# Scan input and output, attention scores and probabilities times values as row or column tiles of the TensorE array

## Chip, cores and metric

The kernel runs on one core of one Trainium2 chip. The metric is the device time in microseconds, the median of the runs shown. All times here are microseconds unless marked ns.

## What is computed

Two layers of a decoder trunk over 256 tokens of width 1024, in float32. Each layer has a SwiGLU feed-forward block (hidden width 2816), then three token mixers that are fed by one projection, then a second feed-forward block, with a layer norm after each of the three. What the change touches lies in two of the mixers:

```python
# state-space mixer: 16 groups of 16 channels, 64 complex states each
bu_re = jnp.einsum('bsgc,gpc->bsgp', uf, bbar_re)      # input of the scan
bu_im = jnp.einsum('bsgc,gpc->bsgp', uf, bbar_im)
_, _, xs_re, xs_im = lax.associative_scan(combine, (aa_re, aa_im, bu_re, bu_im), axis=1)
y = (jnp.einsum('bsgp,gcp->bsgc', xs_re, c_re)          # output of the scan
     - jnp.einsum('bsgp,gcp->bsgc', xs_im, c_im))
...
# sliding-window attention: 8 query heads, 2 key/value heads, head size 64, blocks of 128 tokens
scores = jnp.einsum('bnqhgd,bnkhd->bnhgqk', qb, kk)
...
out = jnp.einsum('bnhgqk,bnkhd->bnqhgd', probs, vv)
```

## The kernel before

The weights come from HBM in chunks of 1 MB into three raw slots, in the order in which they are used, on SyncE's queue. ScalarE (ACT) rounds each chunk to a high part (L710), VectorE (DVE) makes the remainder (L1056), and TensorE (PE) multiplies three times (high by high, high by low, low by high; `project`, L426 to L428, for projections, `accumulate`, L441, for products that sum over the hidden width). A chunk of the projection is 48 matmuls of 256 moving columns. PE's order of work is written out by hand, and each chunk waits for its low part (`take`) and for ACT to have read the PSUM bank that it writes.

The parts of the mixers stand between the chunks of the projection in PE's list. They are plain float32 matmuls, each of which the trace shows as two pairs of a weight load and a matmul record. Their order in one layer is: scores (L606 for the block with a predecessor, 8 matmuls of 256 columns; L610 for the first block, 8 of 128 columns), chunks CC and HH, input 0, BB, chunk 7, input 1, chunk 8, output 0, chunk 9, input 2, transposes of the probabilities, chunk 10, output 1, `attend(1)`, chunk 11, input 3, transposes, chunk 12, output 2, `attend(0)`, chunks 13 and 14, output 3, chunk 15, and the gate of the state-space mixer.

The scan runs over 16 groups of channels, two to a "state tile" of 128 partitions, so eight state tiles; they are done two at a time (q from 0 to 3). `input_states(q)` (L554) makes 4 matmuls: for state tile t and the real or imaginary part, the stationary operand `bTz[:, t, ri, :]` has 128 rows of channels of which only 32 are not zero, and `uT` moves 256 tokens; the results go to PSUM bank 0 or 1. ACT copies them to `bu` (L826), DVE turns them (`turned_parts`, L1275 and L1276), scans (L1295) and turns them back into `sw` (L1304, L1305). `output_states(q)` (L564) makes 4 matmuls that add into one half of bank 2, with `cTz[:, t, ri, :]` stationary, of whose 128 columns only 32 are not zero. ACT may copy the states of q only when `sw` of q-1 is made, and PE waits for `sw` before output q.

For the scores a query tile `qT[:, m, :]` holds two heads, m in partitions 0 to 63 and m+4 in 64 to 127, and `kz` holds the keys of each of the two key heads with zeros in the other half, so 128 rows are multiplied of which 64 count. DVE scales and masks the scores (L1312), reduces them and makes the negative bound (L1359); ACT takes the exponentials (L879); GpSimd (POOL) normalises; PE transposes the probabilities. `attend(blk)` (L588) multiplies `vz[:, kb, j, :]`, which has the values of key head j in 64 of its columns and zeros in the rest, by the transposed probabilities of 128 queries, and sums over both key heads and one or two key blocks: 16 matmuls for block 1, 8 for block 0. ACT reads each gate chunk of the projection out of PSUM with a sigmoid (L818).

Of the kernel before, what the change touches and what calls it, by code (L numbers as in the profile page):

```python
# [27 lines left out]
P = 128  # L28
DEPTH, D, SEQ, DFF = 2, 1024, 256, 2816
# [20 lines left out]
HD, HEADS = 64, 8  # L50
# [55 lines left out]
def trunk(nc, x, ffn1_w_gate, ffn1_w_up, ffn1_w_down, ln1_g, ln1_b, w_in, conv_w, conv_b,  # L106
# [4 lines left out]
    with ctx:  # L111
        def sb(name, shape, dt=F32):
            return ctx.enter_context(nc.sbuf_tensor(name, shape, dt))

        def overlay(first, second):

            size = [sum(4 * math.prod(shape[1:]) for _, shape, _ in s) for s in (first, second)]
            held, brief = (second, first) if size[1] >= size[0] else (first, second)
            with ExitStack() as own:
                over = [own.enter_context(nc.sbuf_tensor(*a)) for a in brief]  # L120
            kept = [sb(*a) for a in held]
            return over + kept if held is second else kept + over
# [13 lines left out]
        probsT, rows_hi, rows_lo = overlay(  # L136
            [("probsT", [P, 2 * HEADS, P], F32)],
            [("rows_hi", [P, 2, 2, SEQ], F32R), ("rows_lo", [P, 2, 2, SEQ], F32R)])
# [7 lines left out]
        bTz, y_cs = overlay([("bTz", [P, STATE_TILES, 2, P], F32)], [("y_cs", [P, 4, 2, SEQ], F32R)])  # L146
# [4 lines left out]
        qT, cv_c, cv_h = overlay([("qT", [P, 4, SEQ], F32)], [("cv_c", [P, 2, SEQ], F32), ("cv_h", [P, 2, SEQ], F32)])  # L151
        kz = sb("kz", [P, 2, SEQ])
        vz = sb("vz", [P, 2, 2, P])
# [11 lines left out]
        sw = sb("sw", [P, 2, 2, SEQ])  # L165
        tp = sb("tp", [P, 2, 2, SEQ])
        k_tok = sw[:, 0, :, 0:P]
        uT = sb("uT", [P, 2, SEQ])
        cTz = sb("cTz", [P, STATE_TILES, 2, P])
# [23 lines left out]
        ps = ctx.enter_context(nc.psum_tensor("ps", [P, 8, 512], F32))  # L193
# [215 lines left out]
        def _(pe):  # L409
            mm = nc.tensor.matmul  # L410
# [98 lines left out]
            with pe.Fori(0, DEPTH) as l:  # L509
# [9 lines left out]
                for u in range(2):  # L519
                    for ri in range(2):  # L520
                        n = (2 * u + ri) * P
                        nc.tensor.transpose(ps[:, 0, n:n + P], b_blk[:, ri, 4 * u:4 * u + 4, :], ident[:, :])
                        last = nc.tensor.transpose(ps[:, 1, n:n + P], c_in[:, u, ri, :, :], ident[:, :])
# [24 lines left out]
                def input_states(q):  # L548

                    if q >= 1:  # L550
                        pe.wait_ge(bu_made.sem, bu_made.at(l, q))
                    for t in range(2 * q, 2 * q + 2):
                        for ri in range(2):
                            last = mm(ps[:, t % 2, ri * SEQ:ri * SEQ + SEQ], bTz[:, t, ri, :], uT[:, t // 4, :],  # L554
                                      start=True, stop=True)
                    last.then_inc(bu_done.sem, 1)

                def output_states(q):

                    pe.wait_ge(x_state_made.sem, x_state_made.at(l, q + 1))  # L560
                    ct = q // 2
                    for t in range(2 * q, 2 * q + 2):
                        for ri in range(2):
                            last = mm(ps[:, 2, ct * SEQ:ct * SEQ + SEQ], cTz[:, t, ri, :], sw[:, ri, t % 2, :],  # L564
                                      start=t % 4 == 0 and ri == 0, stop=t % 4 == 3 and ri == 1)
                    last.then_inc(c_done.sem, 1)

                def transpose_probs(S, parts, g0, first):
# [11 lines left out]
                def attend(blk):  # L580

                    pe.wait_ge(pT_made.sem, pT_made.at(l, 4 if blk else 6))
                    for m in range(4):
                        terms = [(j, kb) for j in range(2) for kb in range(blk + 1)]
                        for n, (j, kb) in enumerate(terms):
                            head = m + 4 * j
                            i = 2 * head + kb if blk else head
                            last = mm(ps[:, 3, m * P:m * P + P], vz[:, kb, j, :], probsT[:, i, :],  # L588
                                      start=n == 0, stop=n == len(terms) - 1)
                    last.then_inc(pv_done.sem, 1)  # L590

                chunk(KV)
# [3 lines left out]
                for t in range(NT):  # L596
                    last = nc.tensor.transpose(ps[:, 2, t * P:t * P + P], k_tok[:, t, :], ident[:, :])
# [4 lines left out]
                pe.wait_ge(proj_read.sem, proj_read.at(l, QB + 1))  # L602
                pe.wait_ge(bcT_made.sem, bcT_made.at(l, 1))
                pe.wait_ge(kz_made.sem, kz_made.at(l, 1))
                for head in range(HEADS):
                    last = mm(ps[:, head // 2, (head % 2) * SEQ:(head % 2) * SEQ + SEQ],  # L606
                              qT[:, head % 4, P:2 * P], kz[:, head // 4, :], start=True, stop=True)
                last.then_inc(scores_done.sem, 1)
                for head in range(HEADS):
                    last = mm(ps[:, 6 + head // 4, (head % 4) * P:(head % 4) * P + P],  # L610
                              qT[:, head % 4, 0:P], kz[:, head // 4, 0:P], start=True, stop=True)
                last.then_inc(scores_done.sem, 1)
                chunk(CC)
                chunk(HH)
                pe.wait_ge(s_made.sem, s_made.at(l, 2))
                input_states(0)
                chunk(BB)
                chunk(7)
                input_states(1)
                chunk(8)  # L620
                output_states(0)
                chunk(9)
                input_states(2)
                pe.wait_ge(probs_made.sem, probs_made.at(l, 1))
                transpose_probs(S1, 4, 0, 0)
                chunk(10)
                output_states(1)
                attend(1)
                chunk(11)
                input_states(3)  # L630
                pe.wait_ge(probs_made.sem, probs_made.at(l, 2))
                transpose_probs(S0, 2, 4, 16)
                chunk(12)
                output_states(2)
                pe.wait_ge(ya_lo.sem, ya_lo.at(l, 1))
                attend(0)
                chunk(13)
                chunk(14)
# [5 lines left out]
                for co in range(2):  # L644
                    for c in range(2):
                        last = mm(ps[:, 0, co * SEQ:co * SEQ + SEQ], w_glu[:, c, co * P:co * P + P], sw[:, 0, c, :],
                                  start=c == 0, stop=c == 1)
# [819 lines left out]
```

## Time and profile before

| | |
|---|---|
| median of 3 runs | 1194.88 (1194.86 to 1196.68) |
| profiled execution | 1195.63, its span 1193.8 |
| busy: PE / DVE / ACT / POOL | 96% / 63% / 48% / 13% |
| mean granted TensorE clock | 0.984 of full speed |
| PE's stretch of the mixers, layer 0 / layer 1 | about 235 to 335 / 822 to 922 |
| HBM | 203.77 MB read, 172 GB/s over the span |

Busy time is the share of the span in which an engine runs an instruction. A matmul record lasts from its start until its last result is written, and the next one starts well before that, so the spacing of starts, and not the duration, is what a matmul takes. In a timeline a row with "x16" merges sixteen neighbouring instructions of one line. An amount in brackets is the idle time of the engine before the instruction and who ended it.

### The profile page before, as it was taken

To read this page: it belongs to the slowest core of one execution; us is meant where nothing else is said; L and a number is where in the kernel's file an instruction comes from. 1 tells how busy PE (TensorE), PEld (TensorE's weight loads), DVE (VectorE), ACT (ScalarE), POOL (GpSimd) and SP (SyncE) were. 2 spreads that over 40 slices of the span, in tenths; PEclk is the share of its full clock that TensorE was granted. 3 is DMA by queue.
4 is the path that set the end of the run, shared out by engine and by line. 5 is a ranking of instruction groups with operands and counts; after the bars stand their busy time and mean duration, and the time that the engine had idled before them with its cause. 6 is when DMAs were issued, how large, how long until landed. Compare 5 with 4: busy or idle time off the path is not lost.

```text
span 1193.8 us, 20955 instructions
## 1 busy us (share of the span) xinstructions
PE 1145.8 (96%) x8164; PEld 1082.6 (91%) x8166; DVE 753.7 (63%) x700; ACT 575.2 (48%) x652; POOL 154.1 (13%) x147
## 2 busy tenths in 40 slices
PE   5999999999999899999979999999999998999995
PEld 5999999999999799999879999989999988999994
DVE  4665447779948664544557544577897586644455
ACT  5565553863444544334356555455735435334331
POOL 2199000003000000000004950000300000000001
PEclk8999999999999899999989999999999998999998
DMA  7565567443466456556455655645445563555650
GB/s 223 181 211 189 192 200 193 155 129 117 139 178 200 153 177 190 195 176 215 139 157 178 207 176 189 232 107 177 141 135 153 174 219 126 191 178 187 197 177 35
DMA packets 176209, 205.60 MB, mean 172 GB/s; under 512 B 27012, under 2 KB 160792, under 8 KB 176152
## 3 DMA queue, kind: packets, MB, share of 16 engines
q1 hardware_dynamic: 175824, 204.76, 54.2%
q8 instruction: 36, 0.59, 0.2%
q14 instruction: 21, 0.17, 0.1%
q10 hardware_dynamic: 328, 0.08, 0.0%
HBM read 203.77 MB, written 1.05 MB: 172 GB/s over the span
## 4 chain that ended last, share of the span: by engine, by line
issue 79%; POOL 13%; PE 6%; ACT 1%; DVE 1%; POOLq 0%; ACTq 0%; DVEq 0%
POOL rot_c L1008 3%; POOL rot_s L1014 2%; POOL tp L1012 2%; POOL S L1022 2%; PE ps L428 1%; PE ps L427 1%; PE ps L426 1%; POOL tp L1010 1%; POOL tp L1004 1%; POOL tp L1006 1%; ACT S L879 1%; PE ps L606 1%; POOL rstd L988 1%; PE ps L543 0%; PE ps L544 0%
## 5 line engine op out<-in xcount | busy, mean ns | idle before, releaser
L1056 DVE TENSOR_TENSOR w_lo<-raw,w_hi 128x2048 fp32r<-128x2048 f32 x186 | 434.4, 2338 | 271.4 <-ACT w_hi L710 271.4
L426 PE MATMUL ps<-xT,w_hi 128*128 128x256 f32 x1984 | 568.1, 286 | 12.8 <-DVE xT L1102 12.8
L427 PE MATMUL ps<-xT,w_hi 128*128 128x256 f32 x1984 | 564.6, 285 | 0.0
L428 PE MATMUL ps<-xT,w_lo 128*128 128x256 f32 x1984 | 564.5, 285 | 0.0
L710 ACT CAST w_hi<-raw 128x2048 fp32r<-128x2048 f32 x186 | 353.4, 1902 | 155.1 <-PE ps L428 114.7
L426 PEld LDWEIGHTS ps<-xT,w_hi 128*128 128x128 f32 x1984 | 384.2, 194 | 17.3 <-DVE xT L1102 15.7
L427 PEld LDWEIGHTS ps<-xT,w_hi 128*128 128x128 f32 x1984 | 384.2, 194 | 1.7
L428 PEld LDWEIGHTS ps<-xT,w_lo 128*128 128x128 f32 x1984 | 383.9, 193 | 0.0
L441 PE MATMUL ps<-w_hi,rows_hi 128*128 128x512 f32 x416 | 130.8, 391 | 0.0
L441 PE MATMUL ps<-w_lo,rows_hi 128*128 128x512 f32 x416 | 130.4, 390 | 0.0
L441 PE MATMUL ps<-w_hi,rows_lo 128*128 128x512 f32 x416 | 130.2, 389 | 0.0
L988 POOL TENSOR_TENSOR rstd<-veps,mhalf 128x1 f32<-128x1 f32 x12 | 6.6, 550 | 815.3 <-DVE veps L1119 815.3
L441 PEld LDWEIGHTS ps<-w_lo,rows_hi 128*128 128x128 f32 x416 | 78.1, 188 | 16.7
L441 PEld LDWEIGHTS ps<-w_hi,rows_lo 128*128 128x128 f32 x416 | 78.1, 188 | 16.6
L721 ACT CAST rows_hi<-hid 128x512 fp32r<-128x512 f32 x44 | 27.3, 620 | 132.3 <-PE ps L441 98.2
L441 PEld LDWEIGHTS ps<-w_hi,rows_hi 128*128 128x128 f32 x416 | 75.3, 189 | 13.1
L715 ACT ACTIVATE act<-ps 128x512 f32<-128x512 f32 x44 | 26.3, 597 | 123.0 <-PE ps L428 122.9
L1069 DVE TENSOR_TENSOR rows_lo<-hid,rows_hi 128x512 fp32r<-128x512 f32 x44 | 32.7, 742 | 57.5 <-ACT rows_hi L721 57.4
L1064 DVE TENSOR_TENSOR hid<-act,ps 128x512 f32<-128x512 f32 x44 | 30.2, 687 | 49.1 <-PE ps L428 49.1
L818 ACT ACTIVATE gates<-ps 128x512 f32<-128x512 f32 x24 | 14.4, 598 | 80.6 <-PE ps L428 80.6
L768 ACT ACTIVATE xTf<-ps,ln_cur 128x128 f32<-128x128 f32 x72 | 27.0, 455 | 9.9 <-PE ps L456 9.9
L1008 POOL TENSOR_TENSOR rot_c<-tp 128x512 f32<-128x512 f32 (+6 forms) x18 | 31.7, 1759 | 1.4
(186 smaller groups left out, 930.4 us busy)
## 6 DMA issues: line engine op xcount, KB each, us to landing
raw<-in_ffn_w_gate SPq DMA_DIRECT2D x44, 1024.0 KB, 5.4
raw<-in_ffn_w_up SPq DMA_DIRECT2D x44, 1024.0 KB, 5.3
raw<-in_ffn_w_down SPq DMA_DIRECT2D x44, 1024.0 KB, 4.9
raw<-in_w_in SPq DMA_DIRECT2D x34, 1024.0 KB, 5.3
raw<-in_w_out SPq DMA_DIRECT2D x8, 1024.0 KB, 4.9
raw<-in_w_in SPq DMA_DIRECT2D x16, 256.0 KB, 4.5
raw<-in_w_br_attn SPq DMA_DIRECT2D x16, 256.0 KB, 4.6
gb<-in_ln_g SPq DMA_DIRECT2D x6, 512.0 KB, 5.3
```

The costliest lines, as they stand in the source:

```text
L426: mm(o, h[:, c, n], xT[:, c, 0, :], start=i == 0, stop=False)
L427: mm(o, h[:, c, n], xT[:, c, 1, :], start=False, stop=False)
L428: last = mm(o, w[:, c, n], xT[:, c, 0, :], start=False, stop=i == KC - 1)
L441: last = mm(acc[:, t, n, :], left[:, buf, c, tok], right[:, c, n * 512:n * 512 + 512], start=start and first and c == 0, stop=stop and lef ...
L710: nc.scalar.copy(w_hi[s][:, :], raw[s][:, :]).then_inc(hi_made.sem, 1)
L715: act_(act[:, :, :], ps[:, 4, :].rearrange("p (m t) -> p m t", m=2), ACT.Silu).then_inc(silu_made.sem, 1)
L721: nc.scalar.copy(rows_hi[:, buf], hid[:, :, :]).then_inc(h_hi.sem, 1)
L768: last = act_(xTf[:, c, t * P:t * P + P], ps[:, 6 - 2 * t + c // 4, (c % 4) * P:(c % 4 + 1) * P], ACT.Identity, scale=ln_cur[:, 2 * (norm_ ...
L1008: tt(rot_c[:, tl, n:2 * n], t0, t1, ALU.subtract).then_inc(pool_chain, 1)
L1056: tt(w_lo[s][:, :], raw[s][:, :], f32(w_hi[s][:, :]), ALU.subtract).then_inc(lo_made.sem, 1)
L1064: tt(hid[:, :, :], act[:, :, :], ps[:, 5, :].rearrange("p (m t) -> p m t", m=2), ALU.mult).then_inc(h_made.sem, 1)
L1069: tt(rows_lo[:, buf], hid[:, :, :], f32(rows_hi[:, buf]), ALU.subtract).then_inc(h_lo.sem, 1)
```

## The change

The zero parts of the operands are no longer multiplied. `input_states` and the scores take the 32 or 64 rows that count, as row tiles of the array; `output_states` and `attend` take the 32 or 64 columns that count, as column tiles. Two column tiles write different partitions of the same bank. The loops are reordered so that two neighbouring matmuls lie in different tiles: state tiles t and t+1 inside the real and the imaginary part; heads m and m+4 in turn; key heads inside key blocks. The count of matmuls and their moving columns stay as they were, and so do all waits and all other engines' work.

```diff
-                    for t in range(2 * q, 2 * q + 2):
-                        for ri in range(2):
-                            last = mm(ps[:, t % 2, ri * SEQ:ri * SEQ + SEQ], bTz[:, t, ri, :], uT[:, t // 4, :],
-                                      start=True, stop=True)
+                    for ri in range(2):
+                        for t in range(2 * q, 2 * q + 2):
+                            ch = slice(32 * (t % 4), 32 * (t % 4) + 32)
+                            last = mm(ps[:, t % 2, ri * SEQ:ri * SEQ + SEQ], bTz[ch, t, ri, :], uT[ch, t // 4, :],
+                                      start=True, stop=True, tile_position=(ch.start, 0))
                     last.then_inc(bu_done.sem, 1)
 
                 def output_states(q):
 
                     pe.wait_ge(x_state_made.sem, x_state_made.at(l, q + 1))
                     ct = q // 2
-                    for t in range(2 * q, 2 * q + 2):
-                        for ri in range(2):
-                            last = mm(ps[:, 2, ct * SEQ:ct * SEQ + SEQ], cTz[:, t, ri, :], sw[:, ri, t % 2, :],
-                                      start=t % 4 == 0 and ri == 0, stop=t % 4 == 3 and ri == 1)
+                    for ri in range(2):
+                        for t in range(2 * q, 2 * q + 2):
+                            ch = slice(32 * (t % 4), 32 * (t % 4) + 32)
+                            last = mm(ps[ch, 2, ct * SEQ:ct * SEQ + SEQ], cTz[:, t, ri, ch], sw[:, ri, t % 2, :],
+                                      start=ri == 0, stop=ri == 1, skip_group_check=True, tile_position=(0, ch.start))
                     last.then_inc(c_done.sem, 1)
...
                     for m in range(4):
-                        terms = [(j, kb) for j in range(2) for kb in range(blk + 1)]
-                        for n, (j, kb) in enumerate(terms):
+                        terms = [(j, kb) for kb in range(blk + 1) for j in range(2)]
+                        for j, kb in terms:
                             head = m + 4 * j
                             i = 2 * head + kb if blk else head
-                            last = mm(ps[:, 3, m * P:m * P + P], vz[:, kb, j, :], probsT[:, i, :],
-                                      start=n == 0, stop=n == len(terms) - 1)
+                            half = slice(HD * j, HD * j + HD)
+                            last = mm(ps[half, 3, m * P:m * P + P], vz[:, kb, j, half], probsT[:, i, :],
+                                      start=kb == 0, stop=kb == blk, skip_group_check=True, tile_position=(0, half.start))
                     last.then_inc(pv_done.sem, 1)
...
-                for head in range(HEADS):
+                by_pairs = [(m + 4 * j, slice(HD * j, HD * j + HD)) for m in range(4) for j in range(2)]
+                for head, half in by_pairs:
                     last = mm(ps[:, head // 2, (head % 2) * SEQ:(head % 2) * SEQ + SEQ],
-                              qT[:, head % 4, P:2 * P], kz[:, head // 4, :], start=True, stop=True)
+                              qT[half, head % 4, P:2 * P], kz[half, head // 4, :], start=True, stop=True,
+                              tile_position=(half.start, 0))
                 last.then_inc(scores_done.sem, 1)
-                for head in range(HEADS):
+                for head, half in by_pairs:
                     last = mm(ps[:, 6 + head // 4, (head % 4) * P:(head % 4) * P + P],
-                              qT[:, head % 4, 0:P], kz[:, head // 4, 0:P], start=True, stop=True)
+                              qT[half, head % 4, 0:P], kz[half, head // 4, 0:P], start=True, stop=True,
+                              tile_position=(half.start, 0))
```

## Rows read from the trace of the kernel before

**Rows 1.** The page: span, busy time by engine, busy tenths of DVE in 40 slices

```profile
span 1193.8 us, 20955 instructions
...
PE 1145.8 (96%) x8164; PEld 1082.6 (91%) x8166; DVE 753.7 (63%) x700; ACT 575.2 (48%) x652; POOL 154.1 (13%) x147
...
DVE  4665447779948664544557544577897586644455
```

**Rows 2.** The page: shares by engine of the chain that ended last

```profile
issue 79%; POOL 13%; PE 6%; ACT 1%; DVE 1%; POOLq 0%; ACTq 0%; DVEq 0%
```

**Rows 3.** Groups of PE by form: busy us, mean ns of one, idle before

```profile
L564 PE MATMUL ps<-sw,cTz 128*128 128x256 f32 x64 | 15.5, 386 | 0.9 <-DVE sw L1305 0.7
L554 PE MATMUL ps<-uT,bTz 128*128 128x256 f32 x64 | 15.1, 379 | 0.0
...
L588 PE MATMUL ps<-probsT,vz 128*128 128x128 f32 x96 | 11.4, 275 | 0.0
```

**Rows 4.** Timeline of PE at the scores, layer 0: start, duration, instruction

```profile
235.73 0.28 PE L428 MATMUL ps<-xT,w_lo 128*128 128x256 f32 x1
235.85 3.62 PE L606 MATMUL ps<-kz,qT 128*128 128x256 f32 x16
239.31 1.95 PE L610 MATMUL ps<-kz,qT 128*128 128x128 f32 x16
241.01 0.36 PE L426 MATMUL ps<-xT,w_hi 128*128 128x256 f32 x1
```

**Rows 5.** Timeline of PE at input 0, layer 0

```profile
252.60 1.89 PE L554 MATMUL ps<-uT,bTz 128*128 128x256 f32 x8
...
254.45 0.28 PE L427 MATMUL ps<-xT,w_hi 128*128 128x256 f32 x1
254.57 0.28 PE L428 MATMUL ps<-xT,w_lo 128*128 128x256 f32 x1
```

**Rows 6.** Timeline of PE at output 1 and attend(1), layer 0

```profile
290.54 0.28 PE L428 MATMUL ps<-xT,w_lo 128*128 128x256 f32 x1
290.92 1.99 PE L564 MATMUL ps<-sw,cTz 128*128 128x256 f32 x8
...
292.75 3.73 PE L588 MATMUL ps<-probsT,vz 128*128 128x128 f32 x32
296.24 0.36 PE L426 MATMUL ps<-xT,w_hi 128*128 128x256 f32 x1
```

**Rows 7.** Timeline of PE at output 3, layer 0

```profile
325.97 1.99 PE L564 MATMUL ps<-sw,cTz 128*128 128x256 f32 x8 [0.35 <-DVE sw L1305]
```

**Rows 8.** Timeline of DVE in the mixers, layer 0

```profile
249.03 0.17 DVE L1359 TENSOR_TENSOR esink<-sinks,negm 128x16 f32<-128x16 f32 x1
...
257.10 2.29 DVE L1056 TENSOR_TENSOR w_lo<-raw,w_hi 128x2048 fp32r<-128x2048 f32 x1 [5.34 <-ACT w_hi L710]
...
269.48 7.83 DVE L1056 TENSOR_TENSOR w_lo<-raw,w_hi 128x2048 fp32r<-128x2048 f32 x2
...
290.18 0.69 DVE L1305 TENSOR_TENSOR sw<-td,tp 128x512 f32<-128x512 f32 x1
...
309.03 2.28 DVE L1056 TENSOR_TENSOR w_lo<-raw,w_hi 128x2048 fp32r<-128x2048 f32 x1
313.97 1.23 DVE L1275 TENSOR_TENSOR td<-bu,rot_c 128x1024 f32<-128x1024 f32 x1 [2.66 <-ACT bu L826]
...
325.23 0.69 DVE L1305 TENSOR_TENSOR sw<-td,tp 128x512 f32<-128x512 f32 x1
```

**Rows 9.** Timeline of ACT in the mixers, layer 0

```profile
247.04 0.59 ACT L813 COPY cv_c<-ps 128x512 f32<-128x512 f32 x1 [8.61 <-PE ps L428]
...
249.45 1.28 ACT L879 ACT_TABLE_LOAD   x1
...
310.63 0.60 ACT L818 ACTIVATE gates<-ps 128x512 f32<-128x512 f32 x1 [5.00 <-PE ps L428]
```

**Rows 10.** After the norm between layers: busy by engine, granted clock; PE's timeline

```profile
600.00:610.00 10.00, 4.50 (x21) 4.50 (x22) 9.93 (x16) 7.88 (x10) 0.00 (x0) 0.67 0.40 112
...
605.88 0.41 PE L427 MATMUL ps<-xT,w_hi 128*128 128x256 f32 x1
606.09 0.41 PE L428 MATMUL ps<-xT,w_lo 128*128 128x256 f32 x1
```

## Prediction, made before the changed kernel ran

> **What bounds the kernel now.** I read the page's busy shares first: PE works 96% of the span and the others far less [rows 1]. So the question is whether a microsecond taken off PE's list comes off the end. The chain of waits doesn't settle it: 79% of it is "issue" [rows 2], PE going from one instruction to the next with nothing to wait for. It says only that PE's order of work is most of the chain. Then the groups of PE instructions: the changed lines have 256 matmul records (64 each for L554 and L564, 96 for L588, and 32 and 32 in two layers for L606 and L610) [rows 3, 4]. An fp32 matmul is two records, each a weight load and a pass. The timeline gives what they take. Sixteen passes of 256 columns run from 235.85 to 239.31, 0.216 each; sixteen of 128 columns from there to 241.01, 0.106 each [rows 4]. The durations in the groups (379 and 275 ns) are latencies of overlapping instructions and are not to be added up. Around an input group of eight passes, L554 starts at 252.60 and the second projection matmul at 254.45; without the group that would be at 252.72, so it costs 1.73, eight times 0.216 [rows 5].
>
> Per layer: eight state groups at 1.73 make 13.8, the scores 3.46 + 1.70 = 5.2, probabilities times values 48 passes of 0.107 = 5.2 (32 of them from 292.75 to 296.24 [rows 6]). That is 24.2 us a layer, 48.4 in all, 4% of the span: all that the change can touch.
>
> Last, what runs beside it. In this stretch DVE is at 9 tenths in two slices of each layer, nearly as full as PE [rows 1]. Its timeline has two idle stretches that matter: 5.34 before 257.10 and 2.66 before 313.97 [rows 8]; between 257.10 and 311.3 it never rests. PE, in its turn, waits for DVE: before the third output group 0.35 [rows 7], and it starts the second 0.26 late (L428 at 290.54, L564 at 290.92 where 290.66 was its turn) [rows 6]. So part of this stretch is bound by DVE's chain and PE's savings are partly lost there.
>
> **The change, part by part.**
>
> Overlap. The operands shrink from 128 partitions or columns to 32 or 64, but the moving columns stay, so a single pass costs what it did (0.216 or 0.107); any gain comes from two tiles running side by side. The program order is tile A pass 1, A pass 2, B pass 1, B pass 2, and matmuls start in order. A's second pass needs A's part of the array, so it waits for A's first; B's first can go beside A's second; B's second waits for B's first and shares its slot with the next A. So n matmuls of alternating tiles take n+1 slots and not 2n (nor n/2 or n/4, though four 32-row tiles exist: neighbours are only ever two tiles). Eight passes become 5 slots, sixteen become 9, thirty-two become 17. Saved: 3 x 0.216 = 0.65 for a state group; 7 x 0.216 + 7 x 0.107 = 1.51 + 0.75 for the scores; 15 x 0.107 = 1.60 for block 1 and 0.75 for block 0 of the values. Neighbours write different banks (row tiles) or different partitions (column tiles), so nothing else separates them.
>
> Switches. Nothing in the trace of before shows a change of tiling. The lower bound is nothing: from L554 to full-size projections there is no gap [rows 5]. The nearest rows for the upper bound are those of the pipeline: a full matmul is 0.28 long but 0.12 after its neighbour, so 0.16 would be laid bare if the array had to empty, and the eight passes after a wait take 1.99 where eight in a stream take 1.89, 0.10 for a weight load that could not be made ahead [rows 5, 6]. Two switches for a state group alone; one each for L610 and L606 (same tile shape, one stretch); three for an output group with its values stretch (32 columns, then 64, then full).
>
> Net on PE per layer: scores 1.51 + 0.75 - 0.52 = 1.74; each of six state groups that stand alone (four input, two output) 0.65 - 0.52 = 0.13; output 1 with block 1 0.65 + 1.60 - 0.78 = 1.47; output 2 with block 0 0.65 + 0.75 - 0.78 = 0.62. Sum 4.6 a layer, 9.2 in all.
>
> Weight loads. Two loads must now fit in a slot. Full loads are seen 0.12 apart (the projections) and here at 0.106 (L610) [rows 4]; two of them make 0.21 to 0.24, as long as a 256-column slot, but twice a 128-column slot. Row tiles keep 128 weight columns, so L610's 0.75 may be zero. That bound goes in the range; column tiles load 32 or 64 columns and are clear of it.
>
> What of it reaches the end. (1) Scores. The DVE waits for L606's last pass (saved 1.51 - 0.26 = 1.25), and ACT for the end of the projection after it, at 247.04 [rows 9] (saved 1.74). DVE's last step of the softmax bound is at 249.03 [rows 8], ACT's exponentials begin at 249.45 [rows 9], so ACT's side is 0.25 later; it leads by 0.5 less after, and the exponentials come about 1.45 earlier. They gate the copy and split that end DVE's idle time at 257.10, and DVE's chain is closed until 290.87, where it releases output 1. PE arrives there 1.74 + 4 x 0.13 = 2.3 early and gains 1.45: about 0.8 is lost as a longer wait before the second output group. The tightest DVE step under way is the rounded-off weights for the projection at 275: two of them take 269.48 to 277.31 [rows 8], so the first is done at 273.4, 1.6 ahead, more than that 0.8. (2) From output 1 to the fourth input: 1.47 + 0.13 = 1.60 ahead of DVE. ACT takes the gate at 310.63 as PE's projection ends, and then copies the last input states, for which DVE idles 2.66 [rows 8, 9]. That idle time covers the 1.60, so all of it counts. (3) From there DVE turns, scans and turns back until PE's third wait at 325.97 [rows 7, 8]: output 2 with block 0, 0.62, is lost. (4) Output 3, 0.13, counts, as PE is alone in front after it. Per layer 1.45 + 1.60 + 0.13 = 3.2; two layers 6.4 us.
>
> The clock. After some norms PE's granted clock is down to 1.2 GHz for a while (0.67 of full speed on average from 600 to 610, when PE had been idle) and matmuls then come 0.21 apart instead of 0.12 [rows 10]. Twenty such records after 605.88 cost 1.9. How many fall under it depends on where the norm lies against these stretches, and everything after 236 moves by microseconds. With five norms to come I allow 2.5 either way and nothing in the middle.
>
> The profiled execution took 1195.63, 1.8 over its span of 1193.8; the median of the three is 1194.88, 0.06% less. 1195.63 - 6.4 = 1189.2; from the median, 1188.5. I predict 1188.5.
>
> **The rivals.**
>
> R1, DVE sets the end. If switches are nearly free, PE runs ahead wherever it can. Then (1) is at most 1.9, (2) would be 0.65 + 1.60 + 0.65 = 2.9 but DVE's idle time ends at 2.66, (4) is 0.65: 5.2 a layer, 1184.5. For it: PE takes other shapes without a gap today. Against: those all use the whole array.
>
> R2, the pairs hardly overlap in the narrow groups, or switches cost some 0.5: then a state group loses 0.35 each, scores keep about 1.2, output 1 with block 1 keeps 0.75, and the sum over both layers is 0 to -2.4: 1192.5 to 1195. It decides where a switch passes 0.32, half of a state group's 0.65.
>
> R3, slower: no two passes overlap. If the second of the two passes holds the whole array, or fp32 passes are not spread over tiles, the slots stay 2n and all 20 switches of a layer are paid at 0.26: 5.2, less the waits before two output groups (0.26 and 0.35) that hide some, about 4.6 a layer, 9.2 in all: 1204. It decides at the first neighbour pair: L606's passes stay 0.216 apart. For it: today two records never run closer than their columns take. Against: today they always share the whole array. The Trainium skill (TensorE: Matmul & The Clock Gate, Part 3) gives 3.07 times for four row tiles of one-pass matmuls and 2.38 for three column tiles, which speaks against R3; no run here shows it for two passes.
>
> R4, the compiler ignores the positions and issues the same full matmuls: the order alone changes and the time is 1194.9. The smaller partitions in the instructions speak against it.
>
> **Chances.** Forecast 0.55, R1 0.12, R2 0.13, R3 0.17, R4 0.03. Within 0.2% (2.4 us, what a measurement of this kernel can tell from no change) lie R4, two thirds of R2, and a forecast upset by the clock. Of R2's rest and of a forecast upset by the clock, 0.02 each go to faster and to slower. Faster 0.67, same 0.14, slower 0.19. The range: R1 less 2 for the clock gives 1182.5; upwards the forecast, R2 and the lower edge of R3 (overlap missing, half of the switch price) give 1200.
>
> **What would show it.** In the profile after: L606 sixteen passes in about 1.9 instead of 3.46, L554 groups in 1.1 (start to start) instead of 1.73, a gap of about 0.26 on either side; PE's lateness before the second output group up from 0.26 to about 1.1, its wait before the last up by 0.6; DVE's idle time for the last input states down from 2.66 to about 1.1. The forecast fails if passes of neighbouring tiles keep the old spacing, if a switch costs over 0.32, or if DVE's idle time doesn't shrink.

## The result, and the profile after

The changed kernel takes 1180.95 (median of 4 runs, 1180.69 to 1182.07) against 1194.87 before (median of 4, 1192.04 to 1196.68). The ratio is 0.9887, with a 95% interval from 0.9867 to 0.9908: 1.1% faster. The profiled execution took 1181.15, with a span of 1179.3, so 14.5 less than the one of before. The forecast was 6.4 less and its range ended at 1182.5, so the measured time lies below the range: right in sign, and the forecast gain is less than half of the measured one.

The page shows PE with 20 us less busy time than in [rows 1], and DVE as it was:

```profile
span 1179.3 us, 20957 instructions
...
PE 1125.3 (95%) x8166; PEld 1055.3 (89%) x8166; DVE 753.4 (64%) x700; ACT 575.1 (49%) x652; POOL 154.0 (13%) x147
```

The timeline of PE at the scores, the counterpart of [rows 4] (L606 and L610 are now L610 and L615):

```profile
235.49 0.28 PE L428 MATMUL ps<-xT,w_lo 128*128 128x256 f32 x1
235.70 2.00 PE L610 MATMUL ps<-kz,qT 64*128 64x256 f32 x16
237.53 1.06 PE L615 MATMUL ps<-kz,qT 64*128 64x128 f32 x16
238.52 0.39 PE L426 MATMUL ps<-xT,w_hi 128*128 128x256 f32 x1
238.74 0.28 PE L427 MATMUL ps<-xT,w_hi 128*128 128x256 f32 x1
```

Sixteen passes of 256 columns went from 3.46 to 1.83, sixteen of 128 columns from 1.70 to 0.99. Read record by record, the passes start in pairs: 0.007 from the first of a pair to the second and 0.209 to the next pair, so 0.216 for two. The passes of 128 columns do the same, with 0.111 for two. So a slot of the prediction, the time of one pass, now holds two. Input 0, the counterpart of [rows 5] (L554 is now L555):

```profile
250.02 0.28 PE L428 MATMUL ps<-xT,w_lo 128*128 128x256 f32 x1
250.23 1.13 PE L555 MATMUL ps<-uT,bTz 32*128 32x256 f32 x8
251.29 0.38 PE L426 MATMUL ps<-xT,w_hi 128*128 128x256 f32 x1
251.51 0.28 PE L427 MATMUL ps<-xT,w_hi 128*128 128x256 f32 x1
```

From the last projection before the group (L428) to the second one after it (L427), 1.49 instead of 1.97. Four slots of 0.216 and the two regular steps of 0.12 make 1.10, so the two changes of tile shape cost 0.39 together, 0.19 each. They are seen as a start that comes 0.21 after L428 and not 0.12, a first pair that is held 0.10 longer, and the same two on the way back.

Output 1 with block 1, the counterpart of [rows 6]:

```profile
286.58 0.28 PE L428 MATMUL ps<-xT,w_lo 128*128 128x256 f32 x1
288.47 1.06 PE L566 MATMUL ps<-sw,cTz 128*32 128x256 f32 x8 [1.61 <-DVE sw L1311]
289.46 1.97 PE L591 MATMUL ps<-probsT,vz 128*64 128x128 f32 x32
291.36 0.39 PE L426 MATMUL ps<-xT,w_hi 128*128 128x256 f32 x1
```

The work from L566 to L426 takes 2.89, where L564 to L426 took 5.32. In front of it PE now idles 1.61 for DVE; before outputs 2 and 3 it idles 0.91 and 0.87. Another 0.5 of its lead goes before that, at the first transposes of the probabilities, where its idle time grows from 0.36 to 0.88. The timeline of DVE, the counterpart of [rows 8]:

```profile
247.27 0.18 DVE L1365 TENSOR_TENSOR esink<-sinks,negm 128x16 f32<-128x16 f32 x1
...
254.64 2.29 DVE L1062 TENSOR_TENSOR w_lo<-raw,w_hi 128x2048 fp32r<-128x2048 f32 x1 [4.98 <-ACT w_hi L716]
...
287.73 0.68 DVE L1311 TENSOR_TENSOR sw<-td,tp 128x512 f32<-128x512 f32 x1
...
306.58 2.28 DVE L1062 TENSOR_TENSOR w_lo<-raw,w_hi 128x2048 fp32r<-128x2048 f32 x1
308.78 1.22 DVE L1281 TENSOR_TENSOR td<-bu,rot_c 128x1024 f32<-128x1024 f32 x1
```

The 2.66 of idle time before the last turn are gone altogether: from 254.64 to 327 DVE has no pause. It is the bound of this stretch now.

Where the 14.5 went, by comparing the starts of the same instructions in the two traces:

| stretch | gain |
|---|---|
| to the scores of layer 0 | 0.15 |
| scores to the last gate (L818, now L824), layer 0 | 5.79 |
| from there to the scores of layer 1 | 1.32 |
| the same stretch in layer 1 | 5.80 |
| from there to the end | 1.42 |

So each layer gave 5.8, and 2.7 came where nothing was changed. The granted clock in windows of 6 us after the second norm of each layer (the one behind the mixers), before and then after. It is the third number from the end of a row, as a share of full speed:

```profile
404.00:410.00 6.00, 5.27 (x28) 4.70 (x27) 5.92 (x6) 4.22 (x4) 0.00 (x0) 0.60 0.15 15
991.00:997.00 6.00, 5.14 (x27) 4.73 (x27) 5.91 (x6) 4.17 (x4) 0.00 (x0) 0.59 0.11 16
```

```profile
397.00:403.00 6.00, 5.18 (x35) 4.05 (x35) 5.77 (x9) 5.44 (x8) 0.00 (x0) 0.90 0.01 3
977.00:983.00 6.00, 5.38 (x36) 4.07 (x34) 5.76 (x9) 5.29 (x7) 0.00 (x0) 0.88 0.01 3
```

Before, 15 and 16 projection matmuls came 0.21 apart there, at 1.2 GHz; after, none did. Each costs 0.093 more at that clock, and 31 times 0.093 is 2.9, near the 2.7. The clock falls at these norms in the changed kernel too, but there it is down only while the transposes and the zeroing of the sum banks run (0.50 from 395.0 to 398.2 in layer 0), and full again when the projection starts at 399.54.

### The profile page after: what moved, and what is told of

It reads as the page before. It is cut to its first block, busy times and chain, and to the rows that moved or that the text cites. A ratio compares the mean times of both kernels' runs of the same rounds, so it can differ in the third digit from the quotient of the medians.

```text
span 1179.3 us, 20957 instructions
## 1 busy us (share of the span) xinstructions
PE 1125.3 (95%) x8166; PEld 1055.3 (89%) x8166; DVE 753.4 (64%) x700; ACT 575.1 (49%) x652; POOL 154.0 (13%) x147
## 4 chain that ended last, share of the span: by engine, by line
issue 79%; POOL 13%; PE 6%; ACT 1%; DVE 1%; POOLq 0%; ACTq 0%; DVEq 0%
POOL rot_c L1014 3%; POOL rot_s L1020 2%; POOL tp L1018 2%; POOL S L1028 2%; PE ps L426 1%; PE ps L428 1%; PE ps L427 1%; POOL tp L1016 1%; POOL tp L1010 1%; POOL tp L1012 1%; ACT S L885 1%; POOL rstd L994 1%; PE ps L543 0%; PE ps L610 0%; PE ps L544 0%
## 5 line engine op out<-in xcount | busy, mean ns | idle before, releaser
L426 PE MATMUL ps<-xT,w_hi 128*128 128x256 f32 x1984 | 566.0, 285 | 12.6 <-DVE xT L1108 12.6
L427 PE MATMUL ps<-xT,w_hi 128*128 128x256 f32 x1984 | 563.1, 284 | 0.0
L428 PE MATMUL ps<-xT,w_lo 128*128 128x256 f32 x1984 | 563.1, 284 | 0.0
L426 PEld LDWEIGHTS ps<-xT,w_hi 128*128 128x128 f32 x1984 | 382.5, 193 | 20.2 <-DVE xT L1108 14.8
L427 PEld LDWEIGHTS ps<-xT,w_hi 128*128 128x128 f32 x1984 | 382.7, 193 | 1.5
L428 PEld LDWEIGHTS ps<-xT,w_lo 128*128 128x128 f32 x1984 | 382.4, 193 | 0.0
L824 ACT ACTIVATE gates<-ps 128x512 f32<-128x512 f32 x24 | 14.3, 598 | 73.9 <-PE ps L428 73.9
```

The lines of the kernel that those rows point to most:

```text
L426: mm(o, h[:, c, n], xT[:, c, 0, :], start=i == 0, stop=False)
L427: mm(o, h[:, c, n], xT[:, c, 1, :], start=False, stop=False)
L428: last = mm(o, w[:, c, n], xT[:, c, 0, :], start=False, stop=i == KC - 1)
```

## The experiments

Two questions were open: how the passes of different tiles run side by side, and what hands PE's gain on to the end. In the tables, "layer" is the gain against the profile of before in that stretch, from the first score matmul to the last gate, for layers 0 and 1, read in the experiment's own trace. The clock after the norms lies outside it. The runs of before were repeated beside each experiment, so their median differs a little from table to table.

### The tiles in the old order

The first hunk stands twice, in `input_states` and in `output_states`.

```diff
-                    for ri in range(2):
-                        for t in range(2 * q, 2 * q + 2):
+                    for t in range(2 * q, 2 * q + 2):
+                        for ri in range(2):
...
-                        terms = [(j, kb) for kb in range(blk + 1) for j in range(2)]
+                        terms = [(j, kb) for j in range(2) for kb in range(blk + 1)]
...
-                by_pairs = [(m + 4 * j, slice(HD * j, HD * j + HD)) for m in range(4) for j in range(2)]
+                by_pairs = [(m + 4 * j, slice(HD * j, HD * j + HD)) for j in range(2) for m in range(4)]
```

> The changed kernel with its tile positions, but the matmuls in the old order: both parts of a state tile, then the next state tile; heads 0 to 3, then 4 to 7; key blocks inside key heads. So runs of 4 (states, block 1 of the values) or 8 passes (scores) of one tile follow one another. In the changed kernel the passes start in pairs 0.007 apart and a pair takes 0.216 (256 columns). Theory F (free tiles): each tile works off its own passes, and program order holds only within a tile. Then the order is of no account, provided that PE looks far enough ahead: L610's sixteen passes still take 1.8, and the time is 1181 +- 1. Theory N (neighbours): a pass can run beside the one before it only. Then a state group takes 7 slots of 8 plus the switches and costs 0.15 more than before, the scores 15 of 16 slots, block 1 about 25 of 32: nothing is gained in the groups but 0.7 in block 1, and the time is 1194 to 1197.

Measured: 1186.28 (1184.36 to 1188.23) beside 1196.32 of the kernel before on the same chip, ratio 0.9914 (0.9893 to 0.9935); layer 4.85 and 4.83. Neither theory gave that. PE's timeline of this run, at input 0 and at the scores:

```profile
250.71 0.28 PE L428 MATMUL ps<-xT,w_lo 128*128 128x256 f32 x1
250.92 1.14 PE L555 MATMUL ps<-uT,bTz 32*128 32x256 f32 x8
251.99 0.39 PE L426 MATMUL ps<-xT,w_hi 128*128 128x256 f32 x1
```

```profile
235.43 2.32 PE L610 MATMUL ps<-kz,qT 64*128 64x256 f32 x13
237.37 0.37 PE L615 MATMUL ps<-kz,qT 64*128 64x128 f32 x1
237.58 0.38 PE L610 MATMUL ps<-kz,qT 64*128 64x256 f32 x1
237.59 0.38 PE L615 MATMUL ps<-kz,qT 64*128 64x128 f32 x2
237.80 0.38 PE L610 MATMUL ps<-kz,qT 64*128 64x256 f32 x1
237.81 0.38 PE L615 MATMUL ps<-kz,qT 64*128 64x128 f32 x2
```

The input group takes what it takes in the changed kernel (1.14 against 1.13), though four passes of one tile come before the first of the other. Theory N is out. At the scores, where eight passes of one tile come first, four run alone (starts 0.22 to 0.32 apart) and the ninth starts 0.007 after the fifth; from there two tiles are at work. The stretch takes 3.79 instead of 2.82, and that 0.97 is the 0.95 that this kernel's layer lacks against 5.80. The rows show even more: L615's passes (they are for the tile that got through first) start ahead of L610 passes that stand before them in the program. So a tile works off its own passes and other tiles don't hold it, within a limit: the ninth pass waits for the fifth, and L615's first, the seventeenth, starts 0.006 after the thirteenth. What the limit counts was not worked out; a plain count of four passes it is not, as the twenty-first starts at 237.92, ahead of the sixteenth at 238.01.

Theory F holds with that limit; its 1181 did not. The limit explains 1.9 of the 5.3 by which the median lies over the changed kernel's. By the traces the difference is 6.3, of which 4.4 lies outside the layers' stretches: after the second norms 16 and 18 projections came 0.21 apart again, and 1.4 was lost at the first norm of layer 1, where neither the kernel before nor the changed one met the lower clock.

### Row tiles alone, column tiles alone

The first has scan output and probabilities times values as before, the second has scores and scan input as before. Their diffs are the halves of the change.

> Row tiles alone (scan input and scores); scan output and probabilities times values as before. By the measured pieces, scores 2.2 less and an input group 0.5 less. Theory D (DVE's chain hands the scores' gain on, then DVE's idle time before the last input states hands on what PE gained since output 1): 2.2 + 0.5 = 2.7 a layer, 5.4 in all, 1189.5 at the same clock; DVE's idle time 2.66 -> 2.2. If PE alone set the end, it would be 2.2 + 4 x 0.5 = 4.2 a layer, 8.4 in all, 1186.5.

> Column tiles alone (scan output and probabilities times values); scores and scan input as before. By the measured pieces, output 1 with block 1 is 2.4 less, output 3 0.7 less, both in front of DVE or alone. Theory D: 2.4 + 0.7 = 3.1 a layer, 6.2 in all, 1188.7 at the same clock; DVE's idle time 2.66 -> 0.3. With rows_only it should add up to about the 11.4 that the two layers of the changed kernel gave, and what is over that (some 3) to neither, as it comes from the clock after the norms. If PE alone set the end, 2 x 0.5 + 2.4 + 1.5 = 4.9 a layer, 9.8 in all, 1185.

| | median | ratio (95%) | layer | DVE idle before the last turn |
|---|---|---|---|---|
| row tiles | 1188.03 | 0.9935 (0.9918 to 0.9952) | 2.83, 2.81 | 2.15 |
| column tiles | 1188.54 | 0.9939 (0.9922 to 0.9956) | 3.16, 3.16 | 0.24 |

DVE's timelines, row tiles and then column tiles:

```profile
311.24 1.22 DVE L1279 TENSOR_TENSOR td<-bu,rot_c 128x1024 f32<-128x1024 f32 x1 [2.15 <-ACT bu L830]
```

```profile
311.39 1.22 DVE L1277 TENSOR_TENSOR td<-bu,rot_c 128x1024 f32<-128x1024 f32 x1 [0.24 <-ACT bu L828]
```

Theory D gave 2.7 and 3.1 a layer and idle times of 2.2 and 0.3; PE alone would have given 4.2 and 4.9. Theory D stands, and the halves add up: 2.8 + 3.2 = 6.0, less 0.2 for DVE's idle time, which the two together would overdraw. The medians (8.3 and 7.8 under their own runs of before) are larger than 5.6 and 6.3. In both traces no projection after the second norms ran at 1.2 GHz, which is worth 2.7; the trace of the column tiles loses 1.4 of that at the first norm of layer 1, where its granted clock is 0.72 from 793 to 799 and that of before is full in the same work, 796 to 802.

### The normalisation of the probabilities on ACT

```diff
+                def scaled_probs(S, blk):
+                    for head in range(HEADS):
+                        last = nc.scalar.mul(S[:, head, :], S[:, head, :], rden[:, blk, head:head + 1])
+                    last.then_inc(probs_made.sem, 1)
...
                 states(1)
+                sc_.wait_ge(rden_made.sem, rden_made.at(l, 1))
+                scaled_probs(S1, 1)
...
                 attn_hi(1, 1)
+                scaled_probs(S0, 0)
...
-                pool.wait_ge(rden_made.sem, rden_made.at(l, 1))
-                normalise(S1, 1, 2 * P)
-                normalise(S0, 0, P)
```

> The changed kernel, with the normalisation of the probabilities moved from POOL (two instructions, 9.4 us) to ACT (16 multiplications by a scalar for each partition, about 0.5 and 0.4 each), S1 after the second input states' copy and S0 after the first value copy. Theory D says that in the changed kernel DVE is the bound from 254 to 325, with PE waiting 1.6, 0.9 and 0.9 before outputs 1 to 3. Two remainders that run beside POOL's normalisation take 7.83 instead of 4.58 and a turn 2.92 instead of 1.22. Without POOL at that time DVE gains some 4.9 a layer, PE's three waits fall to nothing, and the time falls by about 3.3 a layer, 6 in all: 1175. If PE sets the end and its waits are chance, or if ACT becomes the bound through the extra 7 us, nothing is gained or it is slower: 1181 or more.

Measured: 1182.00 (1179.82 to 1183.36), ratio 0.9883 (0.9862 to 0.9903), so by the medians nothing was gained over the changed kernel's 0.9887, and 1175 was missed. The trace says otherwise: layer 7.65 and 7.66, 1.9 more than the changed kernel. DVE's timeline shows both what was expected and why it was not all of 3.3:

```profile
267.28 4.42 DVE L1067 TENSOR_TENSOR w_lo<-raw,w_hi 128x2048 fp32r<-128x2048 f32 x2
271.62 1.22 DVE L1286 TENSOR_TENSOR td<-bu,rot_c 128x1024 f32<-128x1024 f32 x1
...
307.16 1.23 DVE L1286 TENSOR_TENSOR td<-bu,rot_c 128x1024 f32<-128x1024 f32 x1 [3.16 <-ACT bu L832]
```

Two remainders take 4.42, where they took 7.83 beside POOL [rows 8], and the turn 1.22 instead of 2.92. DVE is 5 ahead, and then idles 3.16 for the last input states, whose copy ACT makes only after a gate that waits for PE. The gain of the two layers (3.7) is missing in the time because the clock took it back: after the second norms 19 and 15 projections ran 0.21 apart.

```profile
396.00:402.00 6.00, 4.57 (x21) 4.26 (x21) 5.92 (x7) 4.63 (x5) 0.00 (x0) 0.50 0.14 14
976.00:982.00 6.00, 4.40 (x25) 4.40 (x26) 5.92 (x7) 4.48 (x5) 0.00 (x0) 0.74 0.05 8
```

### PE kept at work at the norms

```diff
+                if t:
+                    for _ in range(10):
+                        mm(ps[:, 4, :], zero_b[:, 0:P], zero_b[:, :], start=True, stop=True)
                 for c in UPPER_FIRST:
...
-                for t in range(NT):
+                for t in list(range(NT)) * (5 if n == 0 else 1):
```

(In `transposes`, before the second token tile, and in `open_acc`.) It was put into the kernel before, into the changed kernel, and into the one with the normalisation on ACT.

> The kernel before, with ten matmuls of zeros (512 columns, bf16) into an unused bank before the second token tile's transposes of each norm, and the zeroing of the sum banks at the start of each layer done five times, so that PE idles less at the norms. Theory C (the clock gave about 3 of the measured 14 us: 15 and 16 matmuls at 0.21 instead of 0.12 after the second norm of each layer in the profile before, none in the one after): with PE kept at work there, before gains about 3 or more, 1190 to 1192, and the change is worth about 11.4 on top of it. If the clock has no part, this kernel is level with before or slower by the added work, 1195 to 1198.

> The changed kernel with the same added zero matmuls. Theory C: most of the clock's loss was already missing, so it gains less than before does, 0 to 2.5: 1178.5 to 1181; the distance to warm_before is 11.4 +- 1. If the 14 us are all the tiles' doing, the distance is 14.

> The changed kernel with the normalisation of the probabilities on ACT and the zero matmuls at the norms. If both gains hold and lie in different stretches, they add: about 1173 to 1175.

| | median (lowest to highest) | ratio to before (95%) | mean clock | layer |
|---|---|---|---|---|
| before, zeros added | 1191.38 (1189.52 to 1193.29) | 0.9967 (0.9954 to 0.9981) | 0.993 | -0.01, 0.01 |
| changed, zeros added | 1179.71 (1179.19 to 1181.58) | 0.9876 (0.9844 to 0.9909) | 0.994 | 5.80, 5.80 |
| and normalisation on ACT | 1175.10 (1174.62 to 1176.53) | 0.9839 (0.9807 to 0.9871) | 0.994 | 7.65, 7.66 |

With the clock nearly level the change is worth 1191.38 - 1179.71 = 11.7, which is twice 5.80 and not 14. The runs of one kernel spread over up to 4.6, so the medians alone would hardly tell 11.7 from 14; the traces do, with 11.6 inside the layers with and without the zeros. Theory C holds. The normalisation on ACT is worth 4.6 on top of that by the medians; the traces show 3.7 of it inside the layers. Its 1175.10 is at the upper end of the 1173 to 1175 expected.

Added matmuls don't remove all of it: in the kernel before with zeros the clock after the second norm is full in layer 0 and down in layer 1; in the changed kernel with zeros it is the other way round, with 17 projections 0.21 apart in layer 0.

```profile
403.00:409.00 6.00, 4.88 (x40) 4.88 (x41) 5.92 (x5) 4.04 (x4) 0.00 (x0) 1.00 0.15 18
988.00:994.00 6.00, 5.11 (x30) 5.11 (x31) 5.76 (x5) 3.80 (x4) 0.00 (x0) 0.72 0.18 32
```

### The last input states copied earlier

On top of the last kernel, one line moved on ACT's list:

```diff
                 probs_out(4, 2)
+                states(3)
                 gate(12)
                 split(l, MIX0 + 15)
-                states(3)
```

> The kernel of act_warm, with the last copy of input states taken by ACT before the gate of the chunk that precedes it and the next split, and not after them. In act_warm DVE idles 3.16 for this copy and PE waits 1.65 before the last output group. Theory D: the states have been in their bank since 298, so the copy can be made as soon as DVE has turned the third pair back; DVE's 3.16 and PE's 1.65 go, 1.65 a layer, 3.3 in all: 1171.5 to 1172.5. If the gate and the split that are now later hold up PE's next chunk instead, the time is 1175 or more.

Measured: 1172.65 (1171.55 to 1173.91), ratio 0.9818 (0.9798 to 0.9838); layer 9.38 and 9.37, which is 1.7 more than with the line in its old place. The layers gained what Theory D said (1.65 each), and the median is 0.15 over the range given. PE's wait before output 3 is gone:

```profile
315.56 0.28 PE L428 MATMUL ps<-xT,w_lo 128*128 128x256 f32 x1
315.76 1.06 PE L569 MATMUL ps<-sw,cTz 128*32 128x256 f32 x8
```

As Theory D said, what DVE waited for, PE waited for too. This is the fastest kernel of the study, 1.8% under the kernel before and 0.7% under the changed one.

### Four tiles at a time

```diff
-                            half = slice(HD * j, HD * j + HD)
-                            last = mm(ps[half, 3, m * P:m * P + P], vz[:, kb, j, half], probsT[:, i, :],
-                                      start=kb == 0, stop=kb == blk, skip_group_check=True, tile_position=(0, half.start))
+                            for part in (slice(HD * j, HD * j + 32), slice(HD * j + 32, HD * j + HD)):
+                                last = mm(ps[part, 3, m * P:m * P + P], vz[:, kb, j, part], probsT[:, i, :],
+                                          start=kb == 0, stop=kb == blk, skip_group_check=True, tile_position=(0, part.start))
```

> The changed kernel with each 64-column matmul of probabilities times values made as two of 32 columns (twice the matmuls, 96 a layer as 192 passes became; the same result). How many tiles can run side by side? If four can, and weight loads keep up, the 64 passes of block 1 take 16 slots of 0.11, 1.7, as the 32 do now, and the time is 1181 at the same clock. If it is two at a time, they take 3.5, and the layer's time grows by that 1.8, since output 1 with block 1 lies on the path: 1184.5.

(The counts in the bracket are wrong there: the matmuls go from 24 to 48 a layer, the passes from 48 to 96.) Measured: 1182.70 (1182.00 to 1184.24), ratio 0.9899 (0.9878 to 0.9920); layer 5.80 and 5.80, to the hundredth that of the changed kernel with half the matmuls. PE's timeline:

```profile
289.11 0.41 PE L566 MATMUL ps<-sw,cTz 128*32 128x256 f32 x2 [1.60 <-DVE sw L1311]
289.21 0.40 PE L591 MATMUL ps<-probsT,vz 128*32 128x128 f32 x3
289.35 0.39 PE L566 MATMUL ps<-sw,cTz 128*32 128x256 f32 x2
...
289.99 1.92 PE L591 MATMUL ps<-probsT,vz 128*32 128x128 f32 x56
291.84 0.39 PE L426 MATMUL ps<-xT,w_hi 128*128 128x256 f32 x1
```

From 289.11 to 291.84 the 8 output passes and 64 value passes take 2.73; the changed kernel takes 2.89 for 8 and 32. Four tiles ran side by side. As both kinds now have 32-column tiles, the values start while the outputs still run. The median is 1.75 over the changed kernel's all the same; by the trace that lies outside the layers, 1.4 of it at the first norm of layer 1, as with the column tiles alone.

## Why the prediction was right in sign and wrong in size

**What can be touched.** 24.2 a layer on PE, with 0.216 and 0.107 for a pass: held. The single pass did cost what it did. (The changed lines have 288 matmul records, 144 a layer, and not 256; and DVE is at 9 tenths in two slices in layer 0 but in only one in layer 1. Nothing in the sum goes by either.)

**The overlap (the step that failed).** The step was "matmuls start in order ... n matmuls of alternating tiles take n+1 slots". They take n. The old order showed why: a tile doesn't wait for passes of another tile that stand before its own, so A's second pass doesn't delay B's first. A state group saves 4 x 0.216 = 0.86 and not 0.65, the scores 8 slots of each kind and not 7, block 1 of the values 16 and not 15. The forecast took the start order seen in a full array for a rule of the engine; the trace of before could not show it for tiles, and a term of "n slots" should have stood as a bound beside "n+1".

**The switch (mis-sized).** 0.26 forecast, 0.19 measured, inside the bounds of 0 and 0.26. The reason given for the upper end, that a part of the array can't hold the weights for both, was not shown by any run. With the overlap, a state group alone gains 0.48 instead of 0.13. That is small in each and large in its effect, as 0.13 was nearly nothing.

The two give, per layer on PE: scores 2.23 (forecast 1.74), output 1 with block 1 2.4 (1.47), output 3 0.74 (0.13; the change of shape on the way in is mostly hidden in the wait for DVE). Put into the forecast's own steps, n slots and 0.19 make about 1.8 for (1), all 2.66 of DVE's idle time for (2) and 0.48 for (4): 4.9 a layer and 9.9 in all, where 6.4 was forecast and the layers gave 11.6. Of the 1.7 left, 0.8 is the misread row under (1) and 0.5 the way into output 3.

**Weight loads.** The doubt about L610's 128 columns was unfounded: L615's full-width loads start in pairs too, 0.007 apart, two in each slot of 0.111.

**(1) Scores to DVE's chain.** Right that DVE's chain hands it on and that the rest turns into PE's wait before output 1: it was 0.26 late there and is now 1.77 late, 1.61 of it idle. But I let DVE's softmax bound hold the exponentials back: 1.45 forecast, 2.2 measured. The row at 249.45 in [rows 9] was read wrongly. It is ACT's table load, and the exponentials of before begin behind it, 1.5 after the bound was ready at 249.20 and not 0.25:

```profile
250.74 0.51 ACT L879 ACTIVATE S<-S,negm 128x256 f32<-128x256 f32 x1
```

ACT's timeline of the changed kernel shows the cover that this gives:

```profile
246.99 1.28 ACT L885 ACT_TABLE_LOAD   x1
248.28 0.51 ACT L885 ACTIVATE S<-S,negm 128x256 f32<-128x256 f32 x1
```

ACT loads its table as soon as it is free, before the bound is there at 247.45, and the exponentials follow at 248.28, 2.46 earlier than before. Of that, 0.24 was there at the last projection before the scores.

**(2) Output 1 to the last input states.** 1.60 forecast, 2.7 measured. PE gained 2.4 + 0.5 = 2.9, and DVE's idle time of 2.66 was used up: the cap that R1 named. **(3)** Output 2 with block 0 came to nothing, as forecast. **(4)** Output 3 (the wait at 325.97, called the third output group there) gave 0.74 instead of 0.13.

**The rivals.** R1 was the true one in what sets the end, 5.2 a layer against 5.8, and its chance of 0.12 was too low. Its condition, switches that are nearly free, did not come true: a switch costs 0.19, and it was the slot less in every group that brought PE far enough ahead. Its 1184.5 fell short by (1), where it was held to 1.9 for the same oversight, and by the clock. R2, R3 and R4 are refuted by the spacing of L610 and L555.

**The clock.** Allowed for with 2.5 either way and nothing in the middle; it gave 2.7. The lower end of the range took only 2 of the 2.5 off R1, but 1182.0 would have missed 1180.95 as well. Without the clock's 2.7 the time would have been near 1183.6, inside the range and still 5 below the forecast: the clock carried it out of the range, the slots, the switches and the misread row made it miss the size. The runs with added zeros separate it. The runs of before themselves spread from 1191.6 to 1198.0 over the study, the fastest at a mean clock of 0.987 and the slowest at 0.982. Why the lower clock ends ahead of the projection at the changed kernel's second norms and not at before's, though PE idles the same 2.74 at them, was not settled; the kernel with the normalisation on ACT met it again.

## What to carry to other kernels

If an operand has zeros in three quarters or half of its rows or columns, a tile costs per pass what the whole array did and gains only by what runs beside it: count slots as passes over the tiles that take turns, add about 0.19 for each change of tile shape, and let the tiles take turns early: runs of four passes of one tile cost nothing here, runs of eight cost 0.97 at the scores. Then look for the engine that feeds the matmuls before handing the gain to the end: here one engine's remaining idle time, read off its timeline, set how much counted, and, once the normalisation had left POOL, moving one copy on ACT gave 3.4 by the traces beside the 11.6 of the whole change. A gain of one or two microseconds near stretches where PE idles can be made or undone by the clock there, so compare stage by stage and not only end by end.

## What the hardware showed that was not expected

- fp32 passes of different tiles start 0.007 apart and out of program order: L615 at 237.37 ahead of L610 at 237.58. How far ahead a pass may start has a limit: after eight passes of one tile, the first of the other started with the fifth and not earlier.
- Four column tiles of 32 columns ran side by side, 72 passes in 2.73, with every weight load kept up.
- A change of tile shape costs 0.19, less than the 0.16 and 0.10 that the forecast put together from [rows 5, 6]. From 32 to 64 columns (L566 to L591) it costs 0.14.
- DVE's remainders took 7.83 for two beside POOL's normalisation and 4.42 without it, and a turn 2.92 and 1.22. Record by record the two engines take turns in the changed kernel's trace: DVE's second remainder starts at 269.17 but ends 2.15 after POOL's first instruction (at 272.71), and the turn starts at 274.78 but ends 1.08 after POOL's second (at 276.62), so each takes after POOL's end about what it takes alone.
- Zero matmuls in the idle time at the norms raised the mean granted clock from 0.984 to 0.993 and took 0.33% off the kernel before.
